# Value pairs made directly with tokens in the rows, and the first squares taken from token rows

## The reference

```
h = rmsnorm(x, norm_mix);  z = h @ w_in                     # 512 pool columns, then 768 each of q, k, v
a = pool_mixer(z[:, :512]) @ w_up_pool
b = attention_branch(z[:, 512:]) @ w_up_attn                # 3 groups of 4 heads of 64, dilations 1, 4, 16
x = x + (sigmoid(g_a) * a + sigmoid(g_b) * b) @ w_out       # gates are h @ w_gate + b_gate
h = rmsnorm(x, norm_ffn)
x = x + (silu(h @ w_ffn_gate) * (h @ w_ffn_up)) @ w_ffn_down
y = rmsnorm(x, norm_final)
```

## Time and profile before

| what | value |
|---|---|
| median of 3 runs | 2524.72 us (2522.41 to 2524.8) |
| the profiled execution | 2521.34 us, of which the span is 2519.3 us |
| mean granted TensorE clock | 0.995 |
| busy share PE, DVE, ACT, POOL | 99%, 51%, 41%, 68% |
| transfers | 353.77 MB, 140 GB/s over the span |

### The profile page before, as it was taken

One profiled execution on the slowest core, in us unless ns is written; L12 is line 12 of the kernel. 1 busy time (PEld: TensorE's weight loads), 2 busy tenths in 40 slices (PEclk: granted clock), 3 DMA queues, 4 the chain that ended last, 5 costly groups with the idle time before them and its releaser, 6 DMA issues. The chain is left out here.

```text
span 2519.3 us, 33326 instructions
## 1 busy us (share of the span) xinstructions
PE 2487.3 (99%) x12084; PEld 2047.3 (81%) x12084; DVE 1294.9 (51%) x1752; ACT 1031.5 (41%) x1984; POOL 1704.9 (68%) x1258
## 2 busy tenths in 40 slices
PE   8899999999999999999999999999999999999998
PEld 7678877888888888888888887788888888888887
DVE  6775555653522222377965845556553222224768
ACT  5323554444533333346462245534453333334445
POOL 5766446644888888755687755574468888887544
PEclk9999999999999999999999999999999999999999
DMA  5245456472233333375453355655522423335644
GB/s 169 76 151 163 141 171 183 162 264 88 85 99 115 101 91 122 101 238 183 143 163 101 105 155 166 171 174 196 209 93 80 125 92 97 120 95 178 184 127 142
DMA packets 334146, 353.77 MB, mean 140 GB/s; under 512 B 38945, under 2 KB 240289, under 8 KB 332449
## 3 DMA queue, kind: packets, MB, share of 16 engines
q1 hardware_dynamic: 332400, 348.39, 44.1%
q10 hardware_dynamic: 1584, 3.26, 0.4%
HBM read 250.20 MB, written 101.38 MB: 140 GB/s over the span
## 5 line engine op out<-in xcount | busy, mean ns | idle before, releaser
L1330 PE MATMUL ps<-S,t_hi 128*128 128x512 f32 (+1 forms) x2280 | 896.9, 393 | 12.4 <-ACT u L1888 8.7
L1332 PE MATMUL ps<-S,t_lo 128*128 128x512 f32 (+1 forms) x2280 | 886.0, 389 | 0.0
L1331 PE MATMUL ps<-S,t_hi 128*128 128x512 f32 (+1 forms) x2280 | 885.1, 388 | 0.0
L1330 PEld LDWEIGHTS ps<-S,t_hi 128*128 128x128 f32 x2280 | 429.2, 188 | 105.0 <-issue 15.4
L1332 PEld LDWEIGHTS ps<-S,t_lo 128*128 128x128 f32 x2280 | 429.0, 188 | 89.1
L1331 PEld LDWEIGHTS ps<-S,t_hi 128*128 128x128 f32 x2280 | 429.5, 188 | 85.2 <-issue 1.0
L1077 POOL TENSOR_TENSOR t_lo<-wraw,t_hi 128x512 fp32r<-128x512 f32 x175 | 235.4, 1346 | 194.6 <-ACT t_hi L1876 192.0
L1077 POOL TENSOR_TENSOR t_lo<-wraw_ff,t_hi 128x512 fp32r<-128x512 f32 x225 | 289.1, 1286 | 78.7 <-ACT t_hi L1876 68.7
L1077 POOL TENSOR_TENSOR t_lo<-R,t_hi 128x512 fp32r<-128x512 f32 x154 | 218.1, 1420 | 177.7 <-ACT t_hi L1876 177.3
L1876 ACT CAST t_hi<-wraw_ff 128x512 fp32r<-128x512 f32 x225 | 139.9, 623 | 364.5 <-PE ps L1332 363.2
L1330 PE MATMUL ps<-t_hi,d_hi 128*128 128x512 f32 x616 | 240.5, 390 | 0.0
(11 more groups left out here) (226 smaller groups left out, 4005.0 us busy)
## 6 DMA issues: line engine op xcount, KB each, us to landing
d_raw<-d_rows SPq DMA_DIRECT2D x154, 256.0 KB, 2.9
d_rows<-act_f SPq DMA_DIRECT2D x110, 256.0 KB, 2.1
wraw_ff<-w_ffn_up SPq DMA_DIRECT2D x44, 512.0 KB, 4.7
R<-w_ffn_down SPq DMA_DIRECT2D x88, 256.0 KB, 3.2
wraw<-w_in SPq DMA_DIRECT2D x40, 512.0 KB, 6.1
sp_rows<-gst SPq DMA_DIRECT2D x80, 256.0 KB, 2.4
wraw_ff<-w_ffn_gate SPq DMA_DIRECT2D x40, 512.0 KB, 4.9
wo_raw<-w_out SPq DMA_DIRECT2D x36, 512.0 KB, 4.2
```

The source lines that it names most:

```text
L1330: nc.tensor.matmul(o_ps, w[0], r[0], start=begins, stop=False, skip_group_check=True)
L1331: nc.tensor.matmul(o_ps, w[0], r[1], start=False, stop=False, skip_group_check=True)
L1332: return nc.tensor.matmul(o_ps, w[1], r[0], start=False, stop=ends, skip_group_check=True)
```

## The change

The two direct pairs are made in one go with the operands the other way round. The stationary operand is 128 tokens of x and the moving operand is a chunk of 128 channels of the 512 weight columns of both pairs, so the result has tokens in the partitions and can be stored without transposes. `direct_run` makes token tiles 0 to 3 (unnormed x), then 4 and 5, then 6 and 7 (normed quarters). The unnormed tiles are scaled by the token's factor in ACT's copy (`copy_direct`). The loads of the weights are 128 x 2 x 512 in four pieces, between the columns of x.

The sums of squares are taken from a second copy of x that has tokens in the rows (`x_rows`), by ACT with its accumulator, so that the adding on DVE and the token sums on PE go. The second half of the tokens comes first; the rows of the first half are loaded when the squares of the second half are done. The order of the engines' work in the opening is new, and S1 and S2 (sum, cast and remainder) stand ahead of the operands of products 14 to 17, or between them. The casts of S3 wait for both third-sums.

```diff
-HALF_DONE = ((1, 3), (2, DIRECT))
+HALVES = (1, 0)
+RUNS = ((0, 1, 2, 3), (4, 5), (6, 7))
+RUN_BANK = (0, 1, 2, 3, 6, 7, 2, 3)
+OPERANDS_FREE = 3
 KIND = {"A11": 0, "S2": 1, "A12": 2, "S3": 3, "S1": 4, "A22": 5, "S4": 6, "A21": 6}
 LOW_KS = [("A11", k) for k in range(4)] + [("A12", k) for k in range(4)]
 HIGH_KS = [("A21", k) for k in range(4)] + [("A22", k) for k in range(4)]
-OPEN_HIS = LOW_KS[:4] + HIGH_KS + LOW_KS[4:] + [(part, i) for part in ("S2", "S1", "S3", "S4") for i in range(2)]
-POOL_OPEN = LOW_KS[:4] + [("A21", 2), ("A21", 3), ("A22", 1), ("A22", 3)]
+OPEN_HIS = HIGH_KS + LOW_KS + [(part, i) for part in ("S1", "S2", "S3", "S4") for i in range(2)]
+POOL_OPEN = [("A21", 2), ("A21", 3), ("A22", 1), ("A22", 3)] + LOW_KS[:4]
 DVE_OPEN = [key for key in OPEN_HIS if key not in POOL_OPEN]
-NORMS = [(0, k) for k in range(4)] + [(1, k) for k in range(KD)] + [(0, k) for k in range(4, KD)]
+NORMS = [(h, k) for h in (1, 0) for k in range(KD)]
...
-WARM = 24
-SQUARED = [(0, p) for p in range(4)] + [(1, p) for p in range(4)]
+WARM = 22
...
+        x_rows = [[at(f"x_rows{h}_{p}", SP_ * p + o, [D]) for p in range(4)] for h, o in enumerate((0, 24576))]
+        squares0 = [at(f"squares0_{p}", SP_ * p + 8192, [D]) for p in range(4)]
...
+        wraw_both = at("wraw_both", WR, [KD, H2])
...
+        def direct_of(t):
+            return (vT[t] if t < 4 else vst_rows[t - 4])[:, :]
...
+        def operand_of(k):
+            return (t_hi + extra_hi)[k % 4 + (k // 4) * (RING + 1)], (t_lo + extra_lo)[k % 4 + (k // 4) * (RING + 1)]
...
-                def rows_of_first(c):
-                    rows = slice(4 * c, 4 * c + 4)
-                    for j, (w, at_c) in enumerate(pair_columns(0)):
-                        sp.dma_start(wraw_of(0, 0)[:, rows, j, :], w[:, rows, at_c:at_c + P]
-                                     ).then_inc(wraw_in[0] if c else first_in, 16)
-                columns(0)
-                rows_of_first(0)
-                columns(1)
-                columns(2)
-                rows_of_first(1)
-                columns(3)
-                load_pair(0, 1)
+                def rows_of_first(p):
+                    at_c = pair_columns(0)[0][1]
+                    sp.dma_start(wraw_both[:, 2 * p:2 * p + 2, :], w_in_c[:, 2 * p:2 * p + 2, at_c:at_c + H2]
+                                 ).then_inc((first_in, wraw_in[0], wraw_in[1], wraw_half)[p], 16)
+                def rows(h, p):
+                    sp.dma_start(x_rows[h][p][:, :], x_t[0, 4 * h + p]).then_inc(rows_in, 16)
+                for p in range(4):
+                    rows_of_first(p)
+                    columns(p)
+                for p in range(4):
+                    rows(1, p)
                 for p in range(4):
                     sp.dma_start(HT[1][p][:, :, :], xt_k[:, 2 * p:2 * p + 2, H2:T]).then_inc(xh_in[p], 16)
+                sp.wait_ge(ssx_ready, 4)
+                for p in range(4):
+                    rows(0, p)
                 sp.wait_ge(t_ready, OPEN_COUNT[3])
                 load_pair(0, 2)
                 sp.wait_ge(t_ready, DIRECT)
                 load_pair(0, 3)
-                for g, c in V_JOBS[0][:2]:
-                    store_v(0, g, c)
-                sp.wait_ge(tr_full, 4)
+                sp.wait_ge(tr_full, 2)
                 load_tables()
-                for g, c in V_JOBS[0][2:6]:
-                    store_v(0, g, c)
+                for t in range(TT):
+                    sp.wait_ge(direct_copied, t + 1)
+                    for g in range(2):
+                        sp.dma_start(v_rows[g, P * t:P * t + P], direct_of(t)[:, 2 * P * g:2 * P * (g + 1)]).then_inc(v_stored[g], 16)
...
-                for q in range(4):
-                    direct_low(0, q)
-                for q in range(4):
-                    direct_low(1, q)
+                for k in range(KD):
+                    direct_low(k)
+                for key in POOL_OPEN[:4]:
+                    open_low(*key)
                 first_pair_sum(0, 2)
                 second_pair_sum(0, 2)
                 third_pair_sum(0, 2)
-                for key in POOL_OPEN:
+                for key in POOL_OPEN[4:]:
                     open_low(*key)
-                for i in range(2):
-                    open_sums("S1", i)
+                for part in ("S1", "S2"):
+                    for i in range(2):
+                        open_sums(part, i)
                 leading_lows(0, 2, (0, 1))
                 for i in range(2):
-                    open_sums("S2", i)
+                    open_sums("S4", i)
                 leading_lows(0, 2, (2, 3))
-                for i in range(2):
-                    open_sums("S4", i)
...
-            def token_sums(h):
-                pe.wait_ge(added, h + 1)
-                for p in range(4):
-                    ins = nc.tensor.matmul(ps[:, 4 + h, 2 * p:2 * p + 2], squared[h][0][:, 0, p * P:(p + 1) * P], ones[:, 0:2],
-                                           start=p == 0, stop=p == 3, skip_group_check=True)
-                ins.then_inc(tr_full, 1)
...
+            def direct_run(run, between):
+                for k in range(KD):
+                    c, kk = divmod(k, 4)
+                    if run == 0:
+                        pe.wait_ge(s_ready, k + 1)
+                        pe.wait_ge(t_ready, OPEN_COUNT[k])
+                    elif run == 1:
+                        open_ready(pe, f"A2{c + 1}", kk)
+                    for t in RUNS[run]:
+                        b = RUN_BANK[t]
+                        if k == 0:
+                            bank_read(b)
+                            last[b] = ("direct_copied", 0, t + 1)
+                        x = [a[k][:, t * P:(t + 1) * P] for a in (raw_hi, raw_lo)] if run == 0 else [
+                            S[:, t - 4, KIND[f"A2{c + 1}"], hl, kk, :] for hl in range(2)]
+                        ins = three(ps[:, b, :], x, [a[:, :] for a in operand_of(k)], k == 0, k == KD - 1)
+                    if run == 2 and k == 3:
+                        ins.then_inc(prod_done, 1)
+                    if k in between:
+                        factor_rows(between[k])
+                ins.then_inc(prod_done, DIRECT - 3 if run == 2 else 1)
             def opening():
                 warm_up()
-                direct_half(0, 0, {6: [(token_sums, 0)]})
-                direct_half(1, 0, {0: [(factor_rows, 0)], 2: [(value_transposes, 0, 0, 0), (value_transposes, 0, 0, 3)],
-                                   4: [(token_sums, 1)], 6: [(factor_rows, 1)]})
-                direct_half(0, 1, {2: [(value_transposes, 0, 1, 0), (value_transposes, 0, 1, 3)]})
-                direct_half(1, 1, {2: [(value_transposes, 0, 0, 2), (value_transposes, 0, 0, 1)]})
+                direct_run(0, {5: 1})
+                direct_run(1, {5: 0})
+                direct_run(2, {})
...
-                act.wait_ge((xl_in, xh_in)[h][p], 16)
-                nc.scalar.activation(squared[h][p][:, :, :], HT[h][p][:, :, :], ACT.Square).then_inc(ssx_ready, 1)
+                act.wait_ge(rows_in, 64 if h else 128)
+                nc.scalar.activation(squares0[p][:, :], x_rows[h][p][:, :], ACT.Square, accum_out=ssx[:, 4 * h + p:4 * h + p + 1]
+                                     ).then_inc(ssx_ready, 1)
             def deviations(h):
-                act.wait_ge(tr_full, 2 * h + 1)
-                nc.scalar.activation(stdx[:, 4 * h:4 * h + 4], ps[:, 4 + h, 0:8:2], ACT.Sqrt, bias=eps[:, :], scale=1.0 / D
-                                     ).then_inc(stdx_ready, 1)
-            def copy_direct(h, n):
-                act.wait_ge(prod_done, HALF_DONE[n][h])
-                for j in range(2):
-                    c = RESULTS.index((h, j))
-                    if n:
-                        act.wait_ge(vt_full, v_job(0, 0, c) + 1)
-                    nc.scalar.copy(vT[c][:, :], ps[:, 2 * n + j, :]).then_inc(direct_copied, 1)
-            def direct_hi(n, q):
-                i = 4 * n + q
-                act.wait_ge(wraw_in[n] if n or q > 1 else first_in, 32)
-                hi, _ = operand_of(n, q)
-                w = wraw_of(0, n)[:, 4 * (q // 2):4 * (q // 2) + 4, q % 2, :]
-                nc.scalar.copy(blocks(hi[:, :]), w).then_inc(thi_ready, DIRECT - 7 if i == 7 else 1)
+                act.wait_ge(ssx_ready, 4 * HALVES.index(h) + 4)
+                c = slice(4 * h, 4 * h + 4)
+                nc.scalar.activation(stdx[:, c], ssx[:, c], ACT.Sqrt, bias=eps[:, :], scale=1.0 / D).then_inc(stdx_ready, 1)
...
+            def copy_direct(t):
+                if t < 4:
+                    act.wait_ge(prod_done, 1)
+                    act.wait_ge(spread_ready, 2)
+                    nc.scalar.activation(direct_of(t), ps[:, RUN_BANK[t], :], ACT.Copy, scale=rstdx[:, t:t + 1]).then_inc(direct_copied, 1)
+                else:
+                    act.wait_ge(prod_done, 2 if t < 6 else DIRECT)
+                    nc.scalar.copy(direct_of(t), ps[:, RUN_BANK[t], :]).then_inc(direct_copied, 1)
```

(110 more changed lines are left out.)

86 lines of the change are left out of this document (17 added, 69 removed).

## The result

| | us, median (lowest to highest, runs) | ratio to before, 95% interval |
|---|---|---|
| before, beside the first comparison | 2524.76 (2522.41 to 2526.46, 4) | |
| changed, first comparison | 2508.67 (2506.79 to 2509.69, 4) | 0.9937 [0.9924, 0.9951] |
| before, beside the second | 2522.46 (2519.90 to 2524.91, 12) | |
| changed, second comparison | 2508.38 (2506.03 to 2511.56, 5) | 0.9945 [0.9931, 0.9958] |

The change makes the kernel 14 to 16 us faster, and the second comparison, with more runs, gives 14.1; the forecast was 10.35 us, 2514.4, and the range ended at 2509.0, 0.33 us above the first measurement. The direction and the place were right, the size was too small. The profiled execution took 2509.43 us, its span 2506.4, 12.9 us less than the 2519.3 of before.

The account below looks back on a forecast made before the run. TensorE bounds the kernel (busy 2487.3 of 2519.3 us); only its opening waits, chiefly for u, could shrink. u's product 10.35 us sooner: 2524.72 - 10.35 = 2514.4 us, range 2509 to 2521.

Parts of the forecast that it names:

- (a): Removed value transposes, scaling, token sums and square additions: what TensorE saves only lengthens its waits, costed at nothing.
- (b): First product: POOL's operand remainder and DVE's raw remainder now meet, about 9.1 us against 9.20, so nothing gained.
- (c): Loads up to the high rows: weights in 2 KB runs bring landing to 21.5 us (20.1 to 21.8) from 21.8.
- (d): High half: four ACT squares at about 1.12 us done at 26.1; TensorE waits 2.1 us, turns factors by 28.0.
- (e): Low half: rows queued at 26.1 us, landed 34.1; spread, waiting for POOL's sum, ends 43.0; factors turned 43.6.
- (f): Low factors to u's product, pair 2: POOL and DVE alternate, 27.0 us of turns, then 4.5; product at 77.3.
- (g): Sum: u's product 10.35 us sooner, then the same low-clock stretch, 8.26 us for two products; fifth product at 85.6.
- A: Rival, slower: TensorE stays at 1.2 GHz in the direct runs, u's product at 101.6 us, time 2538.7; chance 0.04.
- B: Rival, low rows late: five us late gives 2519.4 (chance 0.13), all four loads in series 2525.2 (0.07).
- C: Rival: POOL and DVE don't exclude each other, u's product at 68.6 us, 19 us gained, 2505.7; chance 0.06.

## Why the prediction was wrong in size

**(a)** held: putting 32 transposes back costs nothing. **(b)** held: first product at 9.24 for 9.1.

**(c)** is the step that failed first, a term that was mis-sized: "worth at most 2.1/0.292 - 2.1/0.382 = 1.7 us ... so I take 0.3 of it: 21.5". The first high square began at 20.42, 1.08 sooner, and with the old runs and issues it begins at 22.46: the layout of these loads, run length and number of issues together, is worth 2.04 us. That the first products wait for the first loads was no reason to cut the term, since the rows stand behind all of these loads on one queue.

**(d)**: four squares to the deviation 4.30 us (24.72 - 20.42) for 4.6. The reading of the accumulator lies beside the next square, and the squares begin 1.04 to 1.06 us apart. TensorE waited 0.27 for 2.1 and kept its clock.

**(e)**: rows issued to first square 8.22 for 8.0, to the deviation 6.48 for 6.7: right. The spread was wrong: I let it wait for POOL's second sum of the pair, until 43.0. It came first, at 39.96 for 0.69, and POOL's sum waited (40.00, 1.79 us). From the deviation's start to the spread's end are 1.23 us for 2.2. In all, the low factors were turned at 41.43 for 43.6: 1.38 of these 2.17 us from (c) and (d), 0.97 from the spread, and -0.18 from the rest. (c) had 20.1 as its bound and (d) 1.04 us a square, so both came out within their bounds; the spread's wait for POOL had no bound and no rival.

**(f)** held to 0.1: 33.82 us for 33.7, from the turned factors to the third product, and a shift of the factors by 6.5 us moved the product by 6.5. This was not luck of opposite errors: S3's splits begin 29.31 us after the turned factors for 29.2, and the product 4.51 after that for 4.5. The prediction had u and the operand within 0.15 us of each other; they were within 0.1, with the operand last.

**(g)** was the second mis-sized term: 8.26 us for two products at the stretch of before, measured 7.18. I carried over a stretch that began with the clock already at half (0.76 for the first matmul); here the idle ahead was 2.79 us in place of 8.73, the first matmuls ran at the full level, and the slow ones lie between 76.48 and 79.85. Without any low clock it is 81.71 - 75.03 = 6.68, since POOL's remainder for the fifth product is next.

So 10.35 + 2.17 + 1.08 - 0.12 = 13.48 us, which is 95.91 - 82.43. The spans give 12.9 and the medians 14.1 and 16.1 with intervals of some 3 us either way.

These terms are 3.13 of the 5.73 us by which 2514.4 missed 2508.67. Most of the other 2.6 lies in the starting point. The sum began at 2524.72, the median of three runs, and the 37 runs of the kernel before in the later comparisons have medians of 2522.03 to 2522.46. From these the same sum gives 2511.7 to 2512.1, 3.3 to 3.7 above the 2508.38 of the second comparison and so close to the 3.13 of the terms. The range was missed by the mis-sized terms and a high starting point together; why the first runs were slower is open. The range was also drawn too narrow by its own bounds: 1.4 from (c), 0.3 from (d), 1.5 from (e) and 1.7 from the clock give 2509.5 as the lower end and not 2510.5.

Of the rivals, A fell with the granted clock of 1.00 in every window from 5 to 55 us. With the loads of 512 bytes the idle ahead of the first product was 2.16 us in place of 1.21 and the clock did fall (0.50 in 11 to 13 us), but it was back at 1.00 from 15 us, and the high factors were turned at 28.15, 0.15 us after their spread ended. Of the others, B fell with the rows in after 8.2 us, and C with the two S2 sums of 6.61 us that became 4.66 when DVE's partner instructions went. The prediction worked out only the sum of the two parts of the change; that they add came out of the runs.

## What to carry to other kernels

Where two engines shut each other out, as POOL and DVE do here with instructions of two SBUF inputs, the chain is the sum of both engines' instructions, so count turns. Moving a sum to the engine that makes it faster can pay (3.9 us here), but the order on that engine then decides how much. Size each load term in full when the consumer stands at the queue's end, and ask of every copy that stands behind casts in an engine's program whether its own input was ready long before. The clock that an idle costs is worth only as much as the next wait allows (0.72 us here). And take the starting point of a forecast from more than three runs where the effect is of the size of their spread.

## What the runs showed of the hardware that I had not expected

- Loads of 2 and 4 KB runs move at 402 to 408 GB/s in 13 to 20 us, in both profiled executions of the changed kernel, where the kernel before had 292 in 13 to 15. The Trainium skill, "DMA: Bandwidth & Descriptors", Specifications, gives about 358 GB/s as the HBM limit of a core; the rows here lie above it, with one core at work.
- From 52.5 to 81.9 us of the changed kernel the ends of POOL's and DVE's two-input instructions follow each other strictly by turns (POOL 64.10, DVE 65.18, POOL 66.32, DVE 67.39). Where DVE's spread began 0.04 us ahead of POOL's sum (39.96 and 40.00), the spread took its 0.69 us and the sum 1.79 for 1.30.
- Squares of 1024 columns with an accumulator began 1.04 to 1.06 us apart; the reading of the accumulator, 0.18 us, lay beside the next square.
